# A streaming encoder step on one Trainium2 core: a new product order in the mixing stage, the last table doubling on VectorE, and a new order in the gated unit, the shared expert and the opening of the expert loop

## The reference

```python
p = h @ w_in                                   # (1088,1024) @ (1024,2048)
u, gb, gc, v = split(p)                        # 512 channels each
y_ssm = s5(u)                                  # complex diagonal scan, 32 groups x 64 states
g = gelu(y_ssm); y_ssm = g * sigmoid(g @ w_glu + b_glu)
y_conv = gb * causal_conv3(gc * v)
mixed = concat([rms_norm(y_ssm, beta_ssm), rms_norm(y_conv, beta_conv)])
h = layer_norm(alpha * h + mixed @ w_out)
top_e, w = route(h)                            # 64 experts, 4 of 8 groups, top 6
f = segment_sum(w * expert[top_e](h)) + shared(h)   # SwiGLU, width 256
out = layer_norm(alpha * h + f)
```

## Time before and its profile

| | |
|---|---|
| median of 3 runs | 1461.6 us (1460.74 to 1461.84) |
| profiled execution | 1459.55 us, its span 1457.6 us |
| mean granted TensorE clock | 0.939 of full speed |
| busy share of the span | PE 86%, DVE 77%, ACT 59%, POOL 55% |
| trunk stage, mixing stage | 0 to 101 us, 101 to 339 us |
| gated unit; projection, routing and shared expert | 339 to 387 us; 387 to 637 us |
| expert stage and final LayerNorm | 637 to 1457.6 us |
| chain that ended last | DMA 31%, PE 17%, DVE 3% of the span |

### The profile page before, as it was taken

One profiled execution on the slowest core, in us unless ns is written; L12 is line 12 of the kernel. 1 busy time (PEld: TensorE's weight loads), 2 busy tenths in 40 slices (PEclk: granted clock), 3 DMA queues, 4 the chain that ended last, 5 costly groups with the idle time before them and its releaser, 6 DMA issues.

```text
span 1457.6 us, 23600 instructions
## 1 busy us (share of the span) xinstructions
PE 1259.2 (86%) x6341; PEld 1068.6 (73%) x6341; DVE 1122.4 (77%) x1438; ACT 864.9 (59%) x1035; POOL 807.0 (55%) x636
## 2 busy tenths in 40 slices
PE   4786979995899879869999999999999999999930
PEld 3786979993688767648888888878878787877820
DVE  6925747762779986648999998888979888898838
ACT  7521202205435543238888888878878878787746
POOL 1018666822601235524888887777857676776710
PEclk9898989997899989979999999999999999999975
DMA  9333314358252232467989999999999999999666
GB/s 277 118 92 59 76 29 90 77 26 269 72 185 97 107 130 103 160 218 278 311 322 368 354 328 355 336 358 347 335 342 312 348 321 339 335 345 331 192 197 255
DMA packets 113844, 335.06 MB, mean 230 GB/s; under 512 B 30400, under 2 KB 61120, under 8 KB 89200
## 3 DMA queue, kind: packets, MB, share of 16 engines
q1 hardware_dynamic: 88880, 280.51, 53.8%
q0 software_dynamic: 24464, 53.72, 15.3%
q10 hardware_dynamic: 432, 0.07, 0.0%
HBM read 288.77 MB, written 70.61 MB: 247 GB/s over the span
## 4 chain that ended last, share of the span: by engine, by line
DMA 31%; PE 17%; DVE 3%; issue 1%; SPq 1%; ACT 1%; ACTq 0%; DVEq 0%; POOLq 0%
DMA rt_raw_up<-in_w_up_dram 30%; PE moe_p_gu L2220 10%; PE moe_p_dn L2232 5%; PE moe_p_tr L2244 2%; DVE rt_raw_up L2370 1%; DVE rt_raw_up L2371 1%; SPq L1961 1%; DVE moe_dn_l L2327 1%; DMA rt_raw_up<-acc 1%; DVE rt_raw_up L2377 1%; DVE moe_up_l L2301 0%; DMA acc<-rt_raw_up,moe_idx_t 0%; ACT moe_dn_h L2082 0%; PE moe_p_ht L2252 0%; DMA acc<-moe_y,moe_idx_t 0%
## 5 line engine op out<-in xcount | busy, mean ns | idle before, releaser
L2301 DVE TENSOR_TENSOR moe_up_l<-rt_raw_up,moe_up_h 128x2048 fp32r<-128x2048 f32 x152 | 348.2, 2292 | 84.4 <-ACT moe_up_h L2027 84.2
L2027 ACT ACTIVATE moe_up_h<-rt_raw_up 128x2048 fp32r (+1 forms) x152 | 291.1, 1917 | 40.9 <-DMA rt_raw_up<-in_w_up_dram 40.5
L2220 PE MATMUL moe_p_gu<-moe_up_h,moe_x_h 128*128 128x512 f32 x608 | 241.3, 397 | 4.5 <-DVE moe_up_l L2301 3.5
L2220 PE MATMUL moe_p_gu<-moe_up_l,moe_x_h 128*128 128x512 f32 x608 | 240.8, 396 | 0.0
L2220 PE MATMUL moe_p_gu<-moe_up_h,moe_x_l 128*128 128x512 f32 x608 | 240.8, 396 | 0.0
L2164 POOL DMA_INDIRECT moe_xg<-tok,moe_idx_g x76 | 185.4, 2439 | 60.3 <-POOL moe_idx_g L2161 43.6
L2173 POOL DMA_INDIRECT acc<-moe_y,moe_idx_s x72 | 180.2, 2502 | 61.6 <-POOL moe_idx_s L2170 55.1
L2327 DVE TENSOR_TENSOR moe_dn_l<-rt_raw_dn,moe_dn_h 128x2048 fp32r<-128x2048 f32 x74 | 168.9, 2282 | 0.0
L2170 POOL COPY moe_idx_s<-keep_small 128x1 int32 (+1 forms) x72 | 116.7, 1621 | 58.1 <-ACT moe_y L2060 58.0
L2082 ACT ACTIVATE moe_dn_h<-rt_raw_dn 128x2048 fp32r x74 | 142.0, 1919 | 0.2 <-issue 0.2
L2220 PEld LDWEIGHTS moe_p_gu<-moe_up_h,moe_x_h 128*128 128x128 f32 x608 | 114.6, 188 | 32.8 <-issue 5.0
(11 more groups left out here) (455 smaller groups left out, 2708.3 us busy)
## 6 DMA issues: line engine op xcount, KB each, us to landing
rt_raw_up<-in_w_gate_dram SPq DMA_DIRECT2D x64, 1024.0 KB, 9.2
rt_raw_up<-in_w_up_dram SPq DMA_DIRECT2D x64, 1024.0 KB, 21.6
rt_raw_dn<-in_w_down_dram SPq DMA_DIRECT2D x64, 1024.0 KB, 17.4
acc<-rt_raw_dn SPq DMA_DIRECT2D x18, 512.0 KB, 2.8
co_win<-in_w_in_dram SPq DMA_DIRECT2D x16, 512.0 KB, 5.0
rt_raw_up<-acc SPq DMA_DIRECT2D x12, 512.0 KB, 12.4
resid<-trunk_x SPq DMA_DIRECT2D x9, 512.0 KB
proj_res<-resid SPq DMA_DIRECT2D x9, 512.0 KB, 3.2
```

The costliest lines, as they stand in the source:

```text
L2027: act.activation(up_h[:, par, half, :, :], raw_up[:, bass.ds(slot, 1), half, :, :].rearrange("p a k n -> p (a k) n"), ACT.Copy).then_inc(u ...
L2220: mm = pe.matmul(p_gu[:, par, :].rearrange("p (a n) -> p a n", a=2), x, w, start=(i == 0), stop=(i == len(terms) - 1))
L2301: low = tt(up_l[:, par, half, :, :], raw_up[:, bass.ds(slot, 1), half, :, :].rearrange("p a k n -> p (a k) n"), up_h[:, par, half, :, :].b ...
```

## The change

Five edits. (1) Mixing: a new `MIX_ORDER`; POOL makes six of the seven doublings, and DVE makes the last at the head of `scan(c)`, behind its wait for the tables (`last_level`, six operations on 128x512); `new_cache(c-1)` stands ahead of the tables of c. (2) Gated unit: `w_glu` in four loads between those of `gT`; the first four products run term by term over all four; gelus go channel block by channel block; the convolution's squares go to ACT (`square_y`, 12) with nine adds on DVE; the square sums are made in three groups. (3) The shared expert's low parts go from POOL to DVE, one in each tile 3 to 8; `in_low` and `hidden(0)` move ahead of `choose_experts` and `norm`, `up(1)` ahead of `turn_hid(0)`, `hidden(6)` ahead of `order_experts`. (4) SP no longer waits for the last stores at the end of the output stage; the expert stage waits for them before its first late load and its first scatter. (5) The opening works on the up weights in two halves of the contraction, interleaved with x; `up(0)` starts on the first half, and `turn_x(1)` lies in its middle.

The diff, cut to what the prediction speaks of:

```diff
-MIX_ORDER = [("v", 0), ("T", 0), ("gc", 0), ("S", 0), ("gb", 0), ("Y", 0),
-             ("T", 1), ("v", 1), ("S", 1), ("gc", 1), ("gb", 1), ("Y", 1),
-             ("T", 2), ("v", 2), ("S", 2), ("gc", 2), ("gb", 2), ("Y", 2),
-             ("T", 3), ("v", 3), ("S", 3), ("gc", 3), ("Y", 3), ("gb", 3)]
+MIX_ORDER = [("v", 0), ("T", 0), ("gc", 0), ("v", 1), ("S", 0), ("gb", 0), ("Y", 0),
+             ("T", 1), ("gc", 1), ("gb", 1), ("S", 1), ("v", 2), ("Y", 1),
+             ("T", 2), ("gc", 2), ("gb", 2), ("S", 2), ("v", 3), ("Y", 2),
+             ("T", 3), ("gc", 3), ("S", 3), ("gb", 3), ("Y", 3)]
+TAB_LEVELS = 7
...
-                if c >= 2:
-                    new_cache(c - 2)
                 if c:
+                    new_cache(c - 1)
                     pool.wait_ge(s_app, c)
 
                 link(pool.memset(cos[:, :, 0:1], 1.0))
                 link(pool.memset(sin[:, :, 0:1], 0.0))
-                for lvl in range(7):
+                for lvl in range(TAB_LEVELS - 1):
...
-            new_cache(KH - 2)
...
+            def last_level(c):
+
+                gs = slice(GT * c, GT * (c + 1))
+                n = 1 << TAB_LEVELS - 1
+                er, ei = (bc(x[:, gs, TAB_LEVELS - 1], 2, n) for x in (co.er, co.eis))
+                a, b = (x[:, 0:GT * n].rearrange("p (g k) -> p g k", g=GT) for x in (t1, t2))
+                tt(a, cos[:, :, 0:n], er, ALU.mult)
+                link(tt(b, sin[:, :, 0:n], ei, ALU.mult))
+                link(tt(cos[:, :, n:2 * n], a, b, ALU.subtract))
+                tt(a, sin[:, :, 0:n], er, ALU.mult)
+                link(tt(b, cos[:, :, 0:n], ei, ALU.mult))
+                link(tt(sin[:, :, n:2 * n], a, b, ALU.add))
+
             def scan(c):
                 gs = slice(GT * c, GT * (c + 1))
                 v.wait_ge(s_tab, c + 1)
+                last_level(c)
...
-            sp.dma_start(w_glu[:, :, :], io.w_glu[0].rearrange("(k p) n -> p k n", p=P)).then_inc(s_wg, 16)
+                sp.dma_start(w_glu[:, c, :], io.w_glu[0, c * P:(c + 1) * P, :]).then_inc(s_wg[c], 16)
...
-            sp.wait_ge(s_ysq, 1)
...
-            for k in range(2):
-                sp.wait_ge(s_acc[k], 16 * N_TILES)
...
+            def square_y(n):
+                c, lo, ln = y_parts[n]
+                act.wait_ge(s_yc[c], 16)
+                if n >= N_CH + 2:
+                    act.wait_ge(s_yadd, n - N_CH - 1)
+                dst = sqy[:, n % 2, 0:ln] if c else ssq[:, 1, lo:lo + ln]
+                act.activation(dst, ycT[:, c, lo:lo + ln], ACT.Square).then_inc(s_ysq, 1)
...
-            for j, (raw, hi, lo) in enumerate(SHARED):
-                pool.wait_ge(s_whs, j + 1)
-                pool.tensor_tensor(lo, raw, hi.bitcast(F32), ALU.subtract).then_inc(s_wls, 1)
...
+            def gate_products_first():
+
+                lo, ln = TOK_CHUNKS[0]
+                for k in range(KH):
+                    pe.wait_ge(s_wg[k], 16)
+                    pe.wait_ge(s_gelu, passes.index((0, k)) + 1)
+                    for mo in range(KH):
+                        mm = pe.matmul(pl[:, mo, 0:ln], w_glu[:, k, mo * P:(mo + 1) * P], gn[:, k, lo:lo + ln],
+                                       start=(k == 0), stop=(k == KH - 1))
+                        if k == KH - 1:
+                            mm.then_inc(s_glu, 1)
...
+            def square_sums(g):
+                pe.wait_ge(s_yadd, len(y_parts) - N_CH)
                 pe.wait_ge(s_added, added(len(glu) - 1))
+                if g:
+                    pe.wait_ge(s_rt, g)
                 for part in range(2):
-                    for i in range(N_TILES):
+                    for i in range(N_TILES)[groups[g]]:
...
+                if i == 1:
+                    square_sums(2)
...
+            up(1)
             turn_hid(0)
-            up(1)
...
+            def shared_low(j):
+                raw, hi, lo = SHARED[j]
+                v.wait_ge(s_whs, j + 1)
+                tt(lo, raw, hi.bitcast(F32), ALU.subtract).then_inc(s_wls, 1)
...
             total(LAST, 1)
+            in_low(LAST + 2)
+            hidden(0)
             choose_experts(LAST - 2)
-            in_low(LAST + 2)
             norm(LAST)
-            hidden(0)
 
             hid_low(0)
...
+            hidden(6)
             order_experts()
-            hidden(6)
...
+                sp.wait_ge(rt.stored[k], 16 * N_TILES)
             down(1, down_slot(1), 1, 0)
             sp.wait_ge(x_turned, FIRST)
...
+                    entries = up_entries(1)
+                    up_high_opening(0)
                     x_high(0, 0)
-                    up_high_opening()
+                    up_high_opening(1)
+                    up_high(1, 1, up_high_first(1, 1, entries), 1)
                     x_high(1, 1)
-                    up_high(1, 1, up_high_first(1, 1, up_entries(1)), 1)
...
+                    pe.wait_ge(opened, 1)
...
+                    if isinstance(n, int) and n == 0 and i == len(terms) // 2:
+                        turn_x(1, 1)
+                        wait(pe, up_l_done, 1)
...
-                        x_low(k, k)
-                        up_low(k, k, entry(v, UP, k, UP_SLOTS - 1) if k else 0)
+                    slot = entry(v, UP, 1, UP_SLOTS - 1)
+                    up_low_opening(0)
+                    x_low(0, 0)
+                    up_low_opening(1)
+                    up_low(1, 1, slot)
+                    x_low(1, 1)
```

More of the change, by code:

```diff
@@ L2045, in up_high_first, with up_high_opening @@
                 return slot
-            def up_high_opening():
+            def up_high_opening(q):
                 act.wait_ge(up_in[0], 32)
-                for half in range(2):
-                    up_high(0, 0, 0, half)
+                act.activation(up_h[:, 0, :, opening[q], :], raw_up[:, 0, :, opening[q], :], ACT.Copy).then_inc(up_h_done, 1)
             def silu(n, par):
@@ L2214, in up @@
                 wait(pe, xl_done, n + 1)
-                wait(pe, up_l_done, n + 1)
+                if isinstance(n, int) and n == 0:
+                    pe.wait_ge(opened, 1)
+                else:
+                    wait(pe, up_l_done, n + 1)
                 wait(pe, hid_done, n - 1)
```

100 lines of the change are left out of this document (62 added, 38 removed).

## The result

The changed kernel takes 1443.8 us (median of 4 runs, 1441.06 to 1446.07) beside 1461.72 for the kernel before (4 runs, 1460.74 to 1461.85): ratio 0.9877, interval 0.9863 to 0.9891, 17.9 us faster. The forecast was 1424.1 and 37.5 us, its range 1408 to 1440: the sign is right, the time lies outside. The profiled execution has a span of 1439.2 us, 18.4 less than before.

What follows compares the result with a forecast made beforehand. Limits differ by stage: PE in mixing, DVE in projection, DMAs in the expert loop, where gains ahead only make it start earlier. Terms sum to 37.5 us (12 to 53) off 1459.55: 1422.05, as a median 1424.1, range 1408 to 1440.

Steps and rivals of the forecast that it cites:

- First token tile, +3.5: First tile: square sums in three groups avoid most of 4.2 us of PE's low clock; 3.5 us (0 to 4.5).
- projection: Token tiles: DVE makes six low parts itself instead of being stretched by POOL; 5 us (0 to 6).
- Shared expert, +3, and sort, +1: Shared expert: earlier hidden(0) and up(1) fill PE's wait, 3 us (0 to 6); hidden(6) ahead of sort, 1 (0 to 3).
- Barrier, +2: Barrier before the expert stage: SP's 2.3 us wait for last stores goes under the opening; 2 us (1 to 2.3).
- Mixing, +8: Mixing stage: table waits of 22.2 us go, DVE's doublings and 1.8 for late stores come back; 8 us (2 to 13).
- Gated unit, +12.5: Gated unit: products start on early weight pieces and DVE runs without POOL, so project(0, 0) comes 12.5 us earlier (9 to 14).
- Opening, +2.5: Expert stage's opening: up(0) starts on half the low part, 3.5 us wait goes, turn_x(1) costs 1; 2.5 us (0 to 4).
- own signs of being wrong: DVE's doublings slower than 1 us each, mixing's PE clock under 0.92, or the loop starting earlier without its end.
- the weight stream: Second rival, expert loop: late weight loads wait for x_turned, opening costs 4.3 us instead of giving 2.5; 1431 us, chance 0.09.
- DVE and ACT as the bound: First rival: work taken off POOL lands on DVE and ACT, which are on the path; 1435 us, chance 0.13.
- The doublings: Third rival, mixing stage: DVE's doublings run contended at 2.06 us each, 33 us more; 1457 us, chance 0.04.
- The clock: Fourth rival, mixing stage: each of four PE stalls leaves the whole next tile at half clock; slower, 1476 us, chance 0.04.

Runs made afterwards that it cites:

- first run: Changed kernel with the second tile's residual load moved on SP ahead of the square-sum wait and the shared expert's weights; ratio 0.9786 to the kernel before, median 1433.42 us.
- the ninth: Fifth run's kernel with the shared expert's weights one place later on SP, behind the third tile's residual; ratio 0.9771 to the kernel before, median 1431.22 us.
- seventh run: First run's kernel with the shared expert's six low parts on POOL again; ratio 0.9838 to the kernel before.
- third run: First run's kernel with the shared expert's down(0) moved on PE ahead of the rank product; ratio 0.9811 to the kernel before.
- fifth run: First run's kernel with the shared expert's start in the old order, hidden(6) still ahead of the sort; ratio 0.9787 to the kernel before.
- sixth run: First run's kernel with SP's wait for the last stores put back at the end of the output stage; ratio 0.9805 to the kernel before.
- fourth run: Kernel before with only the mixing edit (product order, last doubling on DVE, new_cache); ratio 0.9923, median 1452.81 us beside 1465.33.
- eleventh run: Kernel before with the new product order and new_cache moved, all seven doublings on POOL; ratio 0.9943.
- eighth run: First run's kernel with the convolution's squares on POOL again, none on ACT and DVE; ratio 0.9876 to the kernel before.
- the second: Changed kernel with the second tile's residual load between SP's wait for the square sums and the 3 MB of weights; ratio 0.9828 to the kernel before.

## Why the prediction was wrong, step by step

**The step that failed** is *First token tile, +3.5*: "In three groups of 12 the sums are as many, but each is short". PE's and ACT's side of it was right. Left out was who else waits for the sums: SP's wait for `s_ss` went from 1 to `SUMS`, and behind it on SP are 3 MB of weights and then the second residual. The forecast put nothing into its sum for this; that line, in the list of an engine that computes nothing, cost 14.8 us where the second tile starts. The first run gives 10.7 of them back in the stretch, and its ratio goes from 0.9877 to 0.9786. On a median of 1461.7 that ratio would be 1430, by estimate, inside the forecast's range. The stretch from `project(0, 0)` to total 17, for which the forecast had 8.5, is 143.0 before, 146.6 with the change, 135.9 in the first run and 133.6 in the ninth: 7.0 and 9.4 gained once the load is on time. The terms *first tile* (4.7 without the sums that only moved) and *projection* (4.1 in six tiles) were near in size, and the seventh run shows the second of them by itself.

**Shared expert, +3, and sort, +1** was the second miss: -1.2. The step was "`up(1)` fills the wait". It does, but PE did not limit that stretch: the wait of 6.85 became one of 6.88 at the rank product, filling that one gained nothing (third run), and DVE waits longer for the transposed rows (fifth run). The new start costs 2.8 us in the changed kernel from total 17 to `hidden(5)` (60.5 for 57.7), so the bound of 0 that the forecast gave was too good. `hidden(6)` ahead of the sort holds: `hidden(5)` to `hidden(8)` takes 35.9 us instead of 37.5, a little more than the sort's 1.

**Barrier, +2** was wrong: the sixth run shows the stores lay beside PE's way to the barrier. The forecast read SP's row and did not look at which engine came last.

**Mixing, +8** was right in size as far as the profiles tell. The 11.5 of the changed kernel is the largest gain: the eleven profiles with this stage's code have 226.3 to 234.6 us, 230.5 in the mean, 7.3 less than the one profile before; the fourth run's medians give 12.5. The stalls are 15.0 as forecast, from doublings of 0.67 to 0.69 us. The payback was there too: from PE's last matmul of the stage to SP's first load of the next it is 6.1 us before and 7.5 with the change (319.5 to 326.98), 1.4 where the forecast had 1.8, though the last stores took 3.64 us to issue instead of 6.13. The coefficient waits went to 1.7, of another owner. The mechanism is shown for the order only: with all doublings on POOL the stage takes 231.2 us (eleventh run), so what moving the last one adds is not shown.

**Gated unit, +12.5** came out at 10.3, and its two causes do not add: without the free DVE the gain is -0.9 (48.8 against 47.9), without the early load 4.4 (43.5), with both 9.7 (38.2 in the same kernel otherwise). The forecast treated them as one chain, which was right. The size fell short because PE's first four products ended at 345.0 (333.00 and 11.97), where the forecast's 353.3, moved by the 12.0 us that the stages ahead gave, has 341.3. A slip in the forecast is half of that: three quarters of the four products are 7.8 us of PE, and only 6.0 lie between the first gelu (344.7) and 350.7. Another part is the clock: from 333 to 337 it was granted at 0.64, and eight matmuls took 4.0 us there, 2.6 at the pace behind it (0.32 each).

**Opening, +2.5**: 2.8. **Loop**: 1.8 longer in that profile, between -1.8 and 1.8 in the others, so nothing is read from it.

None of the forecast's own signs of being wrong appeared: the doublings stay under 1 us, the granted clock of the mixing stage is 0.95 (0.92 before), and the loop and the end both come earlier, by 20.2 and 18.4 us. Its lower bound is also not what the text says of it: with every term at its high end the time is 1408.6, so 1408 takes the whole way and not two thirds.

The rivals: the weight stream absorbs nothing of a gain at the front (fourth run), and its price of 6.8 us for the new opening is not there either: the opening gains 2.8, and the loop stays within 2 us of the loop before in all ten kernels that have it. DVE and ACT as the bound: its time, 1435, was nearest of all, and for the wrong reason: the moved work did gain, in the seventh and eighth run. The doublings are not contended (0.67 to 0.69 us each, 15.0 of wait in four). The clock: nine slow matmuls after 3.74 us of wait, about as after 11.78 (eight), then a granted clock of 1.00; the slower rival falls, and here a third of the wait did not cost less (1.4 us beside 1.3). All four waits of 3.7 us are followed by slow projection matmuls: 9, 11, 12 and 5, which by their starts take 1.4, 1.7, 1.7 and 0.8 us more than at the pace behind them, 5.6 together. In the trace before it is 8 and 13 behind the waits of 11.78 and 10.38, 1.3 and 2.1 us; the forecast takes off 3 for these two in its 1476, with 0.19 as the difference of 0.52 and 0.33. Not every wait has such matmuls behind it: behind one of 1.90 us in the trace before (282.03) the projection matmuls start 0.17 to 0.18 us apart from the second on, at a granted clock of 1.00 (282 to 286).

## What to carry to other kernels

When a wait on a counter is raised (one group to three), list everything that stands behind the waiting instruction on that queue, loads for other consumers above all; a queue that only issues DMAs is a chain like any other (14.8 us here). A wait that disappears says nothing until one knows which engine limits the stretch: fill PE's wait only where PE is last. Two causes on one chain (a late load, a contended engine) have to be taken away together, and an experiment that undoes one of them takes back more than its share: 10.6 and 5.3 us of 9.7 in the gated unit.

## What was not expected of the hardware

A load of 512 KB was used 3.6 us after its issue when no weights were ahead of it (383.07 to 386.64 in the first run), and after the same 3.6 when the 3 MB were issued right behind it (390.30 to 393.90 in the second). Behind them it took 9.7 (389.01 to 398.74 in the changed kernel).

The mixing stage of the same code took 226.3 to 234.6 us in eleven profiles. PE waits 0 to 3.3 us there for the DMA of the lags, and is itself busy for 201.8 us in the changed kernel and up to 207.1 in others (window 101 to 330), at a granted clock of 0.95 and 0.93 there. What sets this off is not shown. It is of the size of the scatter between runs of one kernel; whether it is the same thing is open, since each kernel has one profile.
